# A two-part block: v of the second attention in quarters, the projections' first splits ahead, another opening order

## The reference

```
q, k, v = split(h @ w_qkv)                # 8 heads, two score maps each, v of 128 columns a head
a = softmax(q0 k0 + bias) - lam * softmax(q1 k1 + bias)
o = a @ v
o = rmsnorm(o, subln_g) * (1 - lambda_init)   # over the 128 columns of a head
return o @ w_o
```

```
merged = gate0 * (y_rw @ p_rw) + gate1 * (y_ml @ p_ml)
x = x + merged @ w_out
x = x + peer(rmsnorm(x), ...)             # queries = normed x @ w_q come first
```

## Time and profile before

| | |
|---|---|
| median of 3 runs | 2287.96 us (2287.33 to 2291.81) |
| the profiled execution, its own time | 2287.46 us |
| its span, first to last instruction | 2285.7 us |
| TensorE matmul busy | 2228.9 us, 98% |
| VectorE busy | 1627.2 us, 71% |
| ScalarE busy | 1040.5 us, 46% |
| moved from and to HBM | 361 MB, 158 GB/s |

### The profile page before, as it was taken

How to read it: one execution, slowest core, us unless ns; L and a number is a source line. 1 busy time by engine, 2 the same in 40 slices (tenths; PEclk the granted TensorE clock), 3 DMA queues, 4 the chain that set the end, 5 groups by cost and what they waited for, 6 DMA issues and landing times. The chain is left out here.

```text
span 2285.7 us, 45770 instructions
## 1 busy us (share of the span) xinstructions
PE 2228.9 (98%) x18056; PEld 2095.2 (92%) x18056; DVE 1627.2 (71%) x3097; ACT 1040.5 (46%) x1694; POOL 107.5 (5%) x46
## 2 busy tenths in 40 slices
PE   7999999999999998999899998999999999999998
PEld 7999789999999887999889988999999999888887
DVE  5665768764875575876586576699789975777776
ACT  5444455443544455544363344444444444333333
POOL 0000000000000000000000000088200000000000
PEclk9999999999999998999999999999999999999999
DMA  5563534564456442556332225445444445555554
GB/s 194 174 202 129 175 119 157 175 201 141 167 176 199 138 149 68 182 187 213 120 129 68 83 75 203 148 159 179 147 143 140 139 157 176 193 193 191 189 191 154
DMA packets 99627, 361.08 MB, mean 158 GB/s; under 512 B 11496, under 2 KB 15736, under 8 KB 99328
## 3 DMA queue, kind: packets, MB, share of 16 engines
q1 hardware_dynamic: 99456, 358.65, 46.6%
HBM read 357.55 MB, written 1.05 MB: 157 GB/s over the span
## 5 line engine op out<-in xcount | busy, mean ns | idle before, releaser
L985 DVE TENSOR_TENSOR w_lo<-ring,w_hi 128x1024 fp32r<-128x1024 f32 (+1 forms) x304 | 397.0, 1308 | 214.7 <-ACT w_hi L781 214.1
L781 ACT ACTIVATE w_hi<-ring 128x1024 fp32r<-128x1024 f32 (+1 forms) x304 | 340.7, 1125 | 365.9 <-PE ps L468 333.7
L468 PE MATMUL ps<-x_hi,w_hi 128*128 128x272 f32 (+1 forms) x1568 | 453.9, 289 | 0.9 <-issue 0.3
L468 PE MATMUL ps<-x_hi,w_lo 128*128 128x272 f32 (+1 forms) x1568 | 449.5, 287 | 0.0
L468 PE MATMUL ps<-x_lo,w_hi 128*128 128x272 f32 (+1 forms) x1568 | 448.1, 286 | 0.0
L468 PEld LDWEIGHTS ps<-x_hi,w_hi 128*128 128x128 f32 x1568 | 295.2, 188 | 3.3 <-issue 1.3
L468 PEld LDWEIGHTS ps<-x_lo,w_hi 128*128 128x128 f32 x1568 | 295.8, 189 | 0.1
L468 PEld LDWEIGHTS ps<-x_hi,w_lo 128*128 128x128 f32 x1568 | 295.1, 188 | 0.0
L243 ACT ACTIVATE v_gated_hi<-ring 128x1024 fp32r<-128x1024 f32 x128 | 135.8, 1062 | 213.6 <-PE ps L3132 213.6
L2873 PE MATMUL ps<-tok_hi,u_mid_hi 128*128 128x256 f32 x704 | 204.5, 290 | 0.0
L468 PE MATMUL ps<-hidden_hi,w_hi 128*128 128x272 f32 (+1 forms) x704 | 201.4, 286 | 0.0
(11 more groups left out here) (499 smaller groups left out, 5130.3 us busy)
## 6 DMA issues: line engine op xcount, KB each, us to landing
ring<-in_gate_up SPq DMA_DIRECT2D x176, 512.0 KB, 3.4
ring<-in_peer_v SPq DMA_DIRECT2D x128, 512.0 KB, 3.2
ring<-in_down SPq DMA_DIRECT2D x64, 704.0 KB, 4.1
ring<-in_peer_u_mid SPq DMA_DIRECT2D x88, 512.0 KB, 3.2
ring<-in_w_in SPq DMA_DIRECT2D x46, 512.0 KB, 3.2
ring<-in_peer_u_early SPq DMA_DIRECT2D x40, 512.0 KB, 3.2
ring<-in_project SPq DMA_DIRECT2D x32, 512.0 KB, 4.0
ring<-in_na_qk SPq DMA_DIRECT2D x16, 512.0 KB, 4.2
```

The lines of the kernel that those rows point to most:

```text
L468: mm = nc.tensor.matmul(ps[:, bank, 0:ntok], parts[left][:, slot, t * P:(t + 1) * P], rhs[right][:, k, 0:ntok], start=start and n == 0, st ...
L781: A.activation(parts[0][:, n % SLOTS, 0:width[n]], ring[:, n % SLOTS, 0:width[n]], ACT.Copy).then_inc(hi_done.sem, 1)
L985: V.tensor_tensor(parts[1][:, n % SLOTS, 0:width[n]], ring[:, n % SLOTS, 0:width[n]], parts[0][:, n % SLOTS, 0:width[n]].bitcast(F32), ALU ...
```

## The change

Three places change, and no product is added or left out.

1. Opening. SyncE issues the second piece of h where `ones` stood, and `ones` after item 2. A one-element square root on ScalarE stands first. ScalarE makes split 0 after x_hi 0, split 1 after x_hi 2, split 2 after x_hi 7, then all eight squares. TensorE runs tile 0 and tile 1 for k = 0 to 2, both for k = 3 to 7, then tile 2, then the eight `h_sum`.

2. Second attention. v is made in four items for columns 0 to 511, and two items that hold 256 columns (512 to 767) for four k-steps each; two more such items for 768 to 1023, "the late quarter", are multiplied after slot 15, into banks 6, 7 and 0, between the last scores and transposes. The loop ends at slot 15 on all engines, and the rest is written out. The head norm runs in two batches, heads 0 to 5 and heads 6 and 7; o_turn uses two banks in place of four and stands one step ahead in place of two; there are three buffers for the kept transposes.

3. Projections. The four splits that opened `project` now stand in `mixers`, on ScalarE and VectorE at slots 43 to 46, ahead of ScalarE's tile and phases of the slot and behind VectorE's.

```diff
+        FIRST_SPLITS = {0: 0, 2: 1, 7: 2}
+        FIRST_TILES = ((0, (0, 1, 2)), (1, (0, 1, 2)), (0, (3, 4, 5, 6, 7)), (1, (3, 4, 5, 6, 7)), (2, range(KD)))
+        EARLY_HEADS = 6
...
             item(0)
-            sp.dma_start(ones[:, :], a["ones"]).then_inc(ones_in, 16)
+            sp.dma_start(h[:, 2:4, 0:T], a["h0"][:, 2:4, :]).then_inc(h_in[1], 16)
             item(1)
-            for n in (1, 2, 3):
+            for n in (2, 3):
                 sp.dma_start(h[:, 2 * n:2 * n + 2, 0:T], a["h0"][:, 2 * n:2 * n + 2, :]).then_inc(h_in[n], 16)
             item(2)
+            sp.dma_start(ones[:, :], a["ones"]).then_inc(ones_in, 16)
             item(3)
             sp.dma_start(ident[:, :], a["ident"]).then_inc(loaded.sem, 16)
...
                 if b == 0:
+                    for m, ks in FIRST_TILES:
+                        pe.wait_ge(lo_done.sem, m + 1)
+                        for k in ks:
+                            pe.wait_ge(x_hi, k + 1)
+                            pe.wait_ge(x_lo, k + 1)
+                            mm = products(m, k, k, m, ntok, x, k == 0, k == KD - 1)
+                        if ks[-1] == KD - 1:
+                            mm.then_inc(used, 1)
                     pe.wait_ge(ones_in, 16)
-
-                for k in range(KD):
+                    for k in range(KD):
+                        h_sum(b, k)
+
+                for k in range(KD if b else 0):
...
-                for item in range(8):
+                def quarter_product(item, t, tile, bank, k):
...
+                    for term, (left, right) in enumerate(TERMS):
+                        mm = nc.tensor.matmul(ps[0:n, bank, 0:256], x[left][:, k, t0:t0 + n], parts[right][:, item % SLOTS, 256 * t:256 * t + 256],
+                                              start=(k == 0 and term == 0), stop=(k == KD - 1 and term == 2))
+                    return mm
+
+                for item in range(8 if local else 6):
...
+                    if not local and side:
+                        for t in range(4):
+                            for tile in range(3):
+                                mm = quarter_product(n0 + item, t, tile, 3 + tile, 4 * pair + t)
+                        mm.then_inc(used, 1)
...
-                    if item == 5:
+                    if item == (5 if local else 4):
...
+                        if m >= 6:
+                            pe.wait_ge(taken, taken_qk + 16 + 3)
...
+                n0 = qk_items[i]
...
-                    for slot in range(16, 20):
-                        beside(slot)
...
                     def o_turn(m):
-                        if m % 2 == 0 and m < 8:
+                        if m % 2 == 0:
                             pe.wait_ge(sub_scaled, m // 2 + 1)
-                        if m >= 4:
-                            pe.wait_ge(o_lo_done, UNITS + m - 3)
+                        if m >= 2:
+                            pe.wait_ge(o_lo_done, UNITS + m - 1)
...
+                            mm = nc.tensor.transpose(ps[:, 2 + m % 2, P * tile:P * tile + P], o_tok[:, tile, P * m:P * m + P], ident[:, :])
                         mm.then_inc(o_turned, 1)

+                    def o_step(k):
+                        pe.wait_ge(o_lo_done, UNITS + k + 1)
+                        side_by_side(n0, side_banks, k, ntok, o_parts)
+
+                    scores(14)
+                    pe.wait_ge(lo_done.sem, late0 + 1)
+                    pe.wait_ge(taken, taken_qk + 15)
+                    for t in range(4):
+                        for tile in range(3):
+                            mm = quarter_product(late0, t, tile, LATE_BANKS[tile], t)
+                    mm.then_inc(used, 1)
+                    turn(13)
+                    scores(15)
+                    pe.wait_ge(lo_done.sem, late0 + 2)
+                    for tile in range(3):
+                        for t in range(4):
+                            mm = quarter_product(late0 + 1, t, tile, LATE_BANKS[tile], 4 + t)
+                        mm.then_inc(used if tile == 2 else late_v, 1)
+                    turn(14)
+                    pv(12)
+                    turn(15)
+                    pv(13)
                     o_turn(0)
                     o_turn(1)
-                    for k in range(KD):
-                        pe.wait_ge(o_lo_done, UNITS + k + 1)
-                        if k == 0:
-                            pe.wait_ge(taken, taken_qk + 16)
-                        side_by_side(n0, side_banks, k, ntok, o_parts)
-                        if k + 2 < KD:
-                            o_turn(k + 2)
+                    pv(14)
+                    o_step(0)
+                    pv(15)
+                    for k in range(1, KD):
+                        if k + 1 < KD:
+                            o_turn(k + 1)
+                        o_step(k)
...
-                    if b == 0 and k in (0, 1, 2):
-                        split_hi(k)
+                    if b == 0:
+                        if k in FIRST_SPLITS:
+                            split_hi(FIRST_SPLITS[k])
+                        continue
...
+                if b == 0:
+                    for k in range(KD):
+                        A.activation(sq[:, k, 0:ntok], stem[:, k, 0:ntok], ACT.Square).then_inc(h_squared, 1)
+                    split_hi(n_next)
...
-                    act.wait_ge(sub_squared, UNITS)
-                    A.activation(sub_root, sums, ACT.Sqrt, scale=1.0 / 128, bias=eps).then_inc(sub_std, 1)
-                    for m in range(KD):
+                    def root(heads):
+                        act.wait_ge(sub_squared, 2 * heads.stop)
+                        A.activation(sub_root[:, :, heads], sums[:, :, heads], ACT.Sqrt, scale=1.0 / 128, bias=eps).then_inc(sub_std, 1)
...
+                    exps(14)
+                    split_hi(n0 + 20)
+                    keep_turned(13)
+                    exps(15)
+                    root(slice(0, EARLY_HEADS))
+                    keep_turned(14)
+                    sub_square(12)
+                    keep_turned(15)
+                    sub_square(13)
+                    turned_hi(0)
+                    turned_hi(1)
+                    sub_square(14)
+                    split_hi(n0 + 21)
+                    sub_square(15)
+                    root(slice(EARLY_HEADS, KD))
+                    for m in range(2, KD):
+                        turned_hi(m)
...
+            act.wait_ge(warm_in, 1)
+            A.activation(spare[:, 1:2], spare[:, 0:1], ACT.Sqrt)
...
-                    if b == 0 and k in (0, 1, 2):
-                        split_lo(k)
+                    if b == 0 and k in FIRST_SPLITS:
+                        split_lo(FIRST_SPLITS[k])
...
-                    if k == (KD - 1 if b in (2, 3, 5) else 3):
+                    if k == (KD - 1 if b in (0, 2, 3, 5) else 3):
...
+                    def take_late_v(tile):
+                        n = KEY_TILES[tile][1]
+                        if tile < 2:
+                            dve.wait_ge(late_v, tile + 1)
+                        else:
+                            dve.wait_ge(used, late0 + 2)
+                        V.tensor_scalar(v[0:n, tile, 768:1024], ps[0:n, LATE_BANKS[tile], 0:256], inv_tok[0:n, tile:tile + 1], None, ALU.mult).then_inc(taken, 1)
+
+                    def inverse_root(heads, batch):
+                        dve.wait_ge(sub_std, batch + 1)
+                        link(V.reciprocal(sub_inv[:, :, heads], sub_root[:, :, heads]))
...
-                    for m in range(KD):
+                    soften(14)
+                    norm(14)
+                    soften(15)
+                    split_lo(n0 + 20)
+                    norm(15)
+                    take_late_v(0)
+                    take_late_v(1)
+                    inverse_root(slice(0, EARLY_HEADS), 0)
+                    take_late_v(2)
+                    scale_heads(0)
+                    take_o(12)
+                    scale_heads(1)
+                    take_o(13)
+                    scale_heads(2)
+                    turned_lo(0)
+                    take_o(14)
+                    turned_lo(1)
+                    take_o(15)
+                    split_lo(n0 + 21)
+                    turned_lo(2)
+                    inverse_root(slice(EARLY_HEADS, KD), 1)
+                    scale_heads(3)
+                    for m in range(3, KD):
                         turned_lo(m)
...
+            V.memset(spare[:, 0:1], 1.0).then_inc(warm_in, 1)
...
+            def next_hi(n):
+                act.wait_ge(ring_full[n % SLOTS].sem, 16 * (w_next.fills_before[n % SLOTS] + 1))
+                act.wait_ge(used, NEXT_AT)
+                A.activation(next_parts[0][:, n, :], ring[:, n % SLOTS, 0:D], ACT.Copy).then_inc(hi_done.sem, 1)
+
...
+                if 0 <= slot - NEXT_AT < PROJECT_AHEAD:
+                    next_hi(slot - NEXT_AT)
...
+            def next_lo(n):
+                dve.wait_ge(hi_done.sem, w_next.first + n + 1)
```

(7 more changed lines are left out.)

119 lines of the change are left out of this document (68 added, 51 removed).

## The result

The changed kernel takes 2274.73 us (median of 4 runs, 2274.24 to 2276.14) against 2288.91 (4 runs, 2287.33 to 2291.81) on the same chip: a ratio of 0.9938, 95% interval 0.9925 to 0.9950. That is 14.2 us less by the medians; the span of the profiled execution went from 2285.7 to 2273.0, 12.7 less. Forecast were 10.5 us less.

What follows compares the result with a forecast made beforehand. TensorE, busy for 98% of the span, was taken to bound the kernel. Opening -3.5, second attention -8.0 and -1.0, projections +2.0 sum to -10.5 us: 2277.5 us against the median 2287.96, range 2272.5 to 2283.

Steps and rivals of the forecast that it cites:

- Opening, -3.5 forecast: Opening: steady matmuls start at 11.35 us in place of 14.23, with 63 left in place of 68; -3.5 us.
- The bound of -5: Opening: largest gain allowed, if item 0 lands early and the pieces before 11.35 also warm the clock; -5 us.
- Attention before the tail, -8.0 forecast: Second attention before the tail: 8.6 us for v's quarter that stays, in place of 16.7; taken as -8.0 us.
- Tail, -1.0 forecast: Second attention's tail, from scores(14) to the fourth output tile: 26.6 us in place of 27.6, late quarter included; -1.0 us.
- my layout's 26.6: Tail laid out step by step from scores(14): 24.6 us of work and 2.0 of waits, none longer than 0.75.
- With 2.7 us: Tail: were the table load 2.7 us, not 1.28, pv(12) would start at 11.7, not 10.8, and the term be -8.1.
- Projections, +2.0 forecast: Ahead of P0: the barrier now waits for all four splits, so TensorE starts at 1385.4, not 1383.40; +2.0 us.
- (a): Rival, projections: loads land early, splits fit between the sigmoids, TensorE starts at 1381.1; -2.3 there, 2273.2 us in all; chance 0.12.
- (b): Rival, tail: it keeps half of its waits, as one late hand-over shifts all behind it; 2281.5 us; chance 0.12.
- (c): Rival, opening: gain only 1.5 us, as the second item lands late; 2279.5 us; chance 0.07.
- (e): Rival: a part does nothing, for instance v's quarters cost 0.15 us a matmul, not 0.12; 2281.8 us; chance 0.05.
- (d): Rival, tail: clock falls at scores(15), stays at half until the fourth output tile; +8.9 us, 2296.9 us; chance 0.04.

Runs made afterwards that it cites:

- the two runs that undid one half of the change each: Changed kernel with v's last quarter made ahead of q and k, 2281.03 us; changed kernel with the second attention's norm in one batch, 2278.94 us.
- the first combined kernel: Changed kernel with one projection split ahead, two steps of VectorE's tail exchanged and 30 zero matmuls in the opening: 2268.30 us, ratio 0.9925.
- the one with two splits ahead: Changed kernel with two of the four projection splits beside the gate tiles, the others behind the barrier: 2271.61 us, ratio 0.9930.
- the zero matmuls: Changed kernel with 30 matmuls of zeros in a spare PSUM bank ahead of the first tile: 2271.45 us, ratio 0.9934.

## Why the prediction was right

**Opening, -3.5 forecast, -3.2 in the profile: right, with two of its terms off against each other.** Tile 0 came 0.6 us earlier (taken as 0, at best 1.3), item 1's split at 8.67 (9.0), the gapless stretch at 11.04 (11.35), tile 4 at 25.07 (25.0). What the sum took over unsaid is that the half-speed stretch would be as long as before (4.2 us). It lasted 5.8 us in this execution and 1.2 to 5.8 in the eight with the same opening: the term is -4.2 on average. The bound of -5 "and the pieces before 11.35 also warm the clock" is passed a little by the best one (-5.5). That this profile came within 0.3 us of the forecast is partly luck of the draw.

**Attention before the tail, -8.0 forecast, -9.0 measured.** scores(14) stands 12.2 us earlier, of which 3.2 are the opening's. The 256-column products cost the 0.12 that the nearest row gave. Not counted were q's first matmul, which came 0.68 us behind the last one of v and now comes 0.12 behind it, and a wait of 0.2 in the slots.

**Tail, -1.0 forecast, -1.6 measured, and here I misread a landmark.** The earlier trace rows end with 909.33, which I called the start of the fourth output tile. It is the start of the eighth output step; six o_turns stand between eight steps, and the fourth tile starts nine matmuls further on, at 910.50. Before, the tail was thus 28.8 us from scores(14), not 27.6:

```profile
909.33 0.39 PE L468 MATMUL ps<-o_hi,w_hi 128*128 128x256 f32 x1
...
910.50 0.28 PE L468 MATMUL ps<-o_hi,w_hi 128*128 128x256 f32 x1
```

After the change it is 27.15 against my layout's 26.6: pv(12) at 11.28 (10.8), pv(13) 12.7 (12.1), pv(14) 14.1 (13.35), first output step 15.3 (14.85), step 2 19.4 (18.95). Each was half a microsecond late from pv(12) on, which waited for the last read-out. The waits named were there (0.41, 0.36, 0.60), none above 0.75, and the clock stayed at 1.00. With the landmark read right the layout would have forecast -2.2. Its own last steps do not quite add up either: step 3 at 20.45 and four more of 1.3 us put step 7 at 25.65, and its nine matmuls of 0.12 end at about 26.7, not 26.6. The landmark made the forecast gain 1.2 us too small, the late steps made the real one 0.5 smaller than laid out; that -1.0 came near -1.6 is in part that the two errors lie against each other.

The table load took 1.28 us again, at 877.72, beside TensorE's late products; ScalarE's instruction before it ends 0.02 us ahead and the root starts 0.01 us behind it. The Trainium skill ("ScalarE: Activation LUTs", "What ACT_TABLE_LOAD costs") gives the same 1.28 us for the load itself and reaches its 2.7 us with a drain beside it, for a switch to another set; this trace shows no such drain. With 2.7 us pv(12) would have come at 11.7 by the forecast's working; it came at 11.28, and what it waited for was the read-out.

**Projections, +2.0 forecast, +2.2 measured: right in mechanism and size.** The gap was to grow from 4.3 to 6.3 us from start to start; it is 6.08. What made it is what the working named: ScalarE's splits 2 and 3 make VectorE's last low half the last thing ahead of the barrier. Counted from the last gate matmul, splits 1 to 3, the sigmoids, that low half and P0 stand within 0.4 us of where the working had them. Not in the sum was that TensorE runs at half speed for longer behind it, 5.0 us in place of 3.4.

**Rivals.** (a), that the projections gain, was wrong for four splits and would have been right for one: P0 then starts 1.97 us behind the last gate matmul, within 0.1 of what (a) assumed. (b), (c) and (e) did not happen. (d), the fall of the clock in the tail, did not happen here; the two runs that undid one half of the change each show it, at 0.50 and 0.52, and take 7.1 and 7.7 us more with their idle time. It was nearer than its 0.04 said, and the forecast's ground against it, that no wait would be longer than 0.75 us, was no safeguard: with the norm in one batch the clock fell behind idle pieces of at most 0.49 us. The changed kernel's own tail has waits of 0.41, 0.36 and 0.60 and kept the clock; by how much it was safe no run shows.

**The unchanged stretches.** The median fell by 14.2 us, the span by 12.7 and the stretches of this change by 11.6. The mixers took 251.1 to 256.9 us in the 14 profiled executions, with the same TensorE instructions in all. What differs is how long TensorE was granted half the clock there. Windows of the mixers in the first combined kernel, the changed kernel and the one with two splits ahead (columns as in the earlier trace rows):

```profile
1109.30:1360.40 251.10, 241.03 (x3555) 227.10 (x3556) 182.45 (x330) 115.73 (x177) 0.00 (x0) 0.98 0.30 98
...
1109.50:1364.00 254.50, 243.92 (x3555) 229.68 (x3556) 182.60 (x330) 114.15 (x174) 0.00 (x0) 0.97 0.30 97
...
1109.10:1366.00 256.90, 246.57 (x3554) 232.07 (x3555) 182.54 (x330) 114.21 (x174) 0.00 (x0) 0.96 0.29 96
```

By the trace's clock records the time at half clock in this stretch was 10.5 and 11.5 us in the two executions of 251.1 and 252.0, 16.3 to 18.1 in the seven of 254.4 to 254.9, 21.1 in the kernel before and 22.2 to 23.0 in the four of 256.4 to 256.9; the order is the same in all 14. It does not go with any edit: with four splits ahead it took each of the three lengths. Why the same waits lower the clock for longer in one execution than in another stays open. The mixers' part in the fall of the span, 0.7 us, goes with such a difference (21.1 us at half clock before, 16.6 after), so the forecast is to be held against the 11.6, of which it is 1.1 short.

The part behind the projections took 865.9 to 869.5. Three executions, that of the changed kernel among them, fell to half clock some 17 us into it and lose 1.5 us there; most of the rest of its scatter stands in the last product (349.9 to 353.8 us), without a record of a lower clock, and stays open. The scatter of these two stretches is larger than the effect of most single edits here, so the medians alone (2271.6 to 2273.4 for five of them) would not have told these apart.

## What to carry to other kernels

Idle time of TensorE can cost its length and then a stretch at half clock: ahead of P0 gaps of 3.56 us and more did so each time and gaps of 1.98 us did not, while in a sparse stretch of the tail idle pieces of at most 0.49 us did. So work that is moved into idle time can pay twice; here it did so in full only where no sparse stretch was left (10.6 us for both halves, 2.9 and 3.5 for one), and a change in two halves should be judged with both in. Of the splits made ahead of the barrier only the first paid; the others stood in the way of what the barrier waits for. Where the same stretch scatters between executions, compare its granted clock before looking for a cause in the edits. Where a wait names an engine, look at what that engine itself was waiting for before exchanging its steps.

## What I had not expected of the hardware

After the start the rate of the matmuls is at half for a time that differs from one execution to the next with the same opening: it ended 1.2 to 5.8 us behind the start of the second stretch at 11 us. It goes with the wait between tile 0's nine matmuls and that second stretch. In the three executions where this wait was at most 0.39 us, full rate came at 12.1 to 13.7 us; in the five where it was 0.53 to 0.91, at 15.4 to 16.8. No run changes this wait alone, so that it is the cause is not shown, but the zero matmuls, which fill it and the time ahead of it, do remove the slow stretch. The granted clock of a window does not show it. The window over the slow stretch of the changed kernel says 1.00 (columns: us, busy (x), granted clock, DMA share, GB/s):

```profile
7.90:16.80 8.90, 8.14 (x34) 1.00 0.95 352
```

while from start to start its matmuls of 272 columns take 0.227 us, against 0.125 behind it. The reason is in the trace: the first record of a granted clock stands at 16.7 us in this execution, where the rate rises, and there is none ahead of it; it is the same in the others (18.5 us in the kernel before, 4.2 with the zero matmuls). A window with no record in it shows 1.00. So in the opening the rate has to be read from the matmuls' starts.

Ahead of P0, gaps of 1.98 us from matmul to matmul left the rate full in three executions; gaps of 3.56 and 4.32 us went with 3.4 to 3.6 us at half speed in three. Gaps of 5.98 to 6.33 us, in the eight executions with four splits ahead, were followed by half speed until 4.6 to 5.9 us behind P0's start in seven and 2.9 in one.
